# A bidirectional hybrid encoder layer: half of the first gather made during routing, and whole-expert loads in the last loop

## The reference

```python
scores = jax.nn.sigmoid(x2d @ w_router)              # 256 x 64
choice = scores + router_bias
grp_score = lax.top_k(choice.reshape(T, 8, 8), 2)[0].sum(-1)
_, top_groups = lax.top_k(grp_score, 4)              # 4 of 8 groups
_, idx = lax.top_k(jnp.where(emask, choice, -jnp.inf), 8)
wsel = wsel / wsel.sum(-1, keepdims=True) * ROUTED_SCALE
...
h = jax.nn.silu(xb @ w_gate[e]) * (xb @ w_up[e])     # 1024 -> 256
out = (h @ w_down[e]) * gate[:, None]                # 256 -> 1024
y = y.at[tok].add(out)
...
shared = (jax.nn.silu(x2d @ ws_gate) * (x2d @ ws_up)) @ ws_down
```

## Time and profile before

| | before |
|---|---|
| median of 3 runs | 745.39 us (743.74, 745.39, 745.47) |
| the profiled execution | 744.41 us |
| its span | 742.5 us |
| PE busy, share of the span | 96% |
| DVE, ACT, POOL busy | 35%, 22%, 6% |
| HBM read | 249.27 MB |
| mean granted TensorE clock | 0.993 |

### The profile page before, as it was taken

One profiled execution on the slowest core, in us unless ns is written; L12 is line 12 of the kernel. 1 busy time (PEld: TensorE's weight loads), 2 busy tenths in 40 slices (PEclk: granted clock), 3 DMA queues, 4 the chain that ended last, 5 costly groups with the idle time before them and its releaser, 6 DMA issues.

```text
span 742.5 us, 11168 instructions
## 1 busy us (share of the span) xinstructions
PE 715.2 (96%) x4520; PEld 416.7 (56%) x4520; DVE 260.8 (35%) x639; ACT 164.9 (22%) x345; POOL 48.0 (6%) x65
## 2 busy tenths in 40 slices
PE   7999999999999999999999999999998999999993
PEld 6888888888864455444444445444443445444441
DVE  3401599656757085222112121022211122112225
ACT  1010423407950043211211111111111121111111
POOL 0120020320320020100000000000000000000000
PEclk9999999999999999999999999999999999999998
DMA  8963544544399548999999999999999999999993
GB/s 329 408 210 147 173 169 167 175 169 159 125 375 376 226 160 332 359 391 423 428 418 429 423 432 429 433 426 421 434 425 422 427 430 419 429 425 421 417 405 157
DMA packets 30931, 250.98 MB, mean 338 GB/s; under 512 B 4001, under 2 KB 4785, under 8 KB 10017
## 3 DMA queue, kind: packets, MB, share of 16 engines
q1 hardware_dynamic: 27792, 240.78, 79.3%
q0 software_dynamic: 2432, 8.44, 3.3%
q10 hardware_dynamic: 656, 1.05, 0.5%
HBM read 249.27 MB, written 1.11 MB: 337 GB/s over the span
## 4 chain that ended last, share of the span: by engine, by line
PE 77%; DVE 9%; SPq 6%; DMA 6%; issue 1%; ACT 1%; DVEq 0%
PE bank L1194 22%; PE bank L820 16%; PE bank L1262 9%; PE bank L1112 8%; PE bank L963 7%; DMA arena<-in_we_dram 5%; PE bank L1132 5%; DVE arena L1585 5%; SPq L627 3%; PE bank L934 1%; PE bank L900 1%; SPq L636 1%; PE bank L1236 1%; PE bank L1271 1%; ACT bank L1350 1%
## 5 line engine op out<-in xcount | busy, mean ns | idle before, releaser
L1194 PE MATMUL bank<-arena 128*64 128x512 f32 (+2 forms) x1008 | 198.7, 601 | 3.7 <-DMA arena<-in_we_dram 3.7
L820 PE MATMUL bank<-arena 128*128 128x256 f32 x768 | 167.7, 379 | 0.0
L820 PEld LDWEIGHTS bank<-arena 128*128 128x128 f32 x768 | 145.6, 190 | 20.5 <-issue 0.4
L1194 PEld LDWEIGHTS bank<-arena 128*64 128x64 f32 (+2 forms) x1008 | 57.7, 127 | 95.6 <-issue 92.9
L1262 PE MATMUL bank<-arena 128*64 128x512 f32 (+2 forms) x512 | 91.7, 584 | 3.3 <-DMA arena<-in_we_dram 1.8
L1112 PEld LDWEIGHTS bank<-onehotb,h_part 128*128 128x128 bf16 x1248 | 69.9, 98 | 20.1 <-issue 20.0
L1112 PE MATMUL bank<-onehotb,h_part 128*128 128x128 bf16 x1248 | 74.3, 219 | 0.2 <-DVE onehotb L1815 0.2
L1903 DVE TENSOR_TENSOR y_lo<-bank,y_hi 128x512 fp32r<-128x512 f32 (+1 forms) x51 | 34.7, 680 | 101.8 <-ACT y_hi L1495 75.5
L1880 DVE TENSOR_REDUCE arena<-bank 64x1 f32<-64x3 f32 (+1 forms) x64 | 10.1, 158 | 160.4 <-PE bank L1212 159.8
L1262 PEld LDWEIGHTS bank<-arena 128*64 128x64 f32 (+1 forms) x512 | 26.2, 124 | 53.7 <-issue 44.6
L963 PE MATMUL bank<-arena 128*128 128x512 f32 x128 | 55.3, 592 | 0.0
(11 more groups left out here) (274 smaller groups left out, 489.8 us busy)
## 6 DMA issues: line engine op xcount, KB each, us to landing
arena<-in_we_dram SPq DMA_DIRECT2D x82, 1024.0 KB, 17.9
arena<-in_we_dram SPq DMA_DIRECT2D x17, 3072.0 KB, 30.2
arena<-in_we_dram SPq DMA_DIRECT2D x22, 2048.0 KB, 30.7
arena<-in_wc_dram SPq DMA_DIRECT2D x15, 1024.0 KB, 11.4
arena<-in_wn_dram SPq DMA_DIRECT2D x8, 1024.0 KB, 4.7
arena<-in_wo_dram SPq DMA_DIRECT2D x8, 1024.0 KB, 4.8
apart<-in_we_dram SPq DMA_DIRECT2D x7, 1024.0 KB, 27.9
arena<-decay_rows POOLq DMA_DIRECT2D x5, 1024.0 KB, 7.1
```

The lines of the kernel that those rows point to most:

```text
L820: mm = nc.tensor.matmul(bank[n % 2][:, j * S:(j + 1) * S], wk, xk, start=(k == 0), stop=(k == KD - 1))
L1194: mm = nc.tensor.matmul(bank[0][rows[q], :], hc[v][:, k, rows[q]], place[at_q[part][q]][:, c:c + 512], start=(k == 0), stop=(k == KD - 1))
```

## The change

**Routing.** The ranks of the first half of the tokens are made as soon as their experts are chosen, in a bank of their own (bank 7). `before` now has 256 on its diagonal, so that a chosen token's rank comes out of the matmul already marked, and the one-hot of a half can be made by one VectorE instruction from PSUM (`first_one_hot`). The one for t = 0 stands inside `top_k(1)`; the first half's 24 matmuls of gather 0 (`gather_of(0, ...)`) are issued while `top_k(1)` runs. After the second ranks come its one-hot and the other 24. The matmuls of `idle_front` go, but for the first 6. `prefixes` moves from the middle of the gather to behind it, and is now float32, with its two matrices loaded with `pk`; `jobs_b` and its cast go. `token_tables` moves from before k = 0 to k = 2 of batch 0, and `job_tables` from k = 2 to k = 3. The h residuals' matmuls use banks 4 and 5.

**Loads.** In the loop each expert of batches 21 to 25 is one load of its three thirds (two, where its places are not side by side); batch 26 keeps single thirds and pieces. And SP waits, for each load, only for the place that is given back last.

```diff
-TABLES_K = 2
-PREFIX_K = 2
-ROUTE_PE = (6, 1, 3)
+TABLES_K = 3
+ROUTE_PE = 6
...
             if closes(b, turn) or (turn is None and b < PAIRED_FROM):
                 return [[(part, q)] for part in range(PARTS) for q in range(w)]
-            if turn is not None or b < WHOLE_FROM:
+            if turn is None and b < WHOLE_FROM:
                 return [[(0, q), (1, q)] for q in range(w)] + [[(2, q)] for q in range(w)]
             return [[(part, q) for part in range(PARTS)] for q in range(w)]
...
+        def waits_for(b, turn, parts, q):
+            if turn is None:
+                return [max(parts, key=lambda p: given_back[True, b, p, q])]
+            return sorted({max(parts, key=lambda p: given_back[at, b, p, q]) for at in (False, None)})
...
-                    for p, _ in whole[::-1]:
-                        if turn is not None or uses(b, turn, p, q):
-                            sp.wait_ge(free[home(b, turn, p, q)], uses(b, turn, p, q))
+                    for p in waits_for(b, turn, [p for p, _ in whole], q):
+                        sp.wait_ge(free[home(b, turn, p, q)], uses(b, turn, p, q))
...
+            def ranks(t):
+                pe.wait_ge(sel_bf, t + 1)
+                to = bank[7][:, 0:E] if t == 0 else bank[3][:, 0:E]
+                for i in range(t + 1):
+                    mm = nc.tensor.matmul(to, (before if i == t else onesb)[:], selb[:, i, :],
+                                          start=(i == 0), stop=(i == t))
+                mm.then_inc(rank_ready, 1)
...
-                if half == 1:
-                    idle_front(ROUTE_PE[1])
...
-            idle_front(ROUTE_PE[2])
             pe.wait_ge(h_part2, 2 * T)
             pe.wait_ge(onehot_ready, 1)
-            gather(0, 0, within=PREFIX_K)
-            gather(0, 1)
-            token_tables()
+            for half in range(2):
+                gather_of(1, half).then_inc(gather_ready, 1)
+            prefixes()
...
+                    if first and k == TABLES_K - 1:
+                        token_tables()
...
+            def first_one_hot(t, marked_rank):
+                dve.wait_ge(rank_ready, t + 1)
+                return V.scalar_tensor_tensor(out=onehotb[0][:, t, :].rearrange("p (e m) -> p e m", e=2),
+                                              in0=marked_rank.unsqueeze(2).to_broadcast([P, 2, M]), scalar=-255.0,
+                                              in1=iota[:, 0:M].unsqueeze(1).to_broadcast([P, 2, M]),
+                                              op0=ALU.add, op1=ALU.is_equal)
...
+                if t == 1:
+                    first_one_hot(0, bank[7][:, 0:2]).then_inc(first_hot, 1)
...
-            one_hot(0, 0, 2, rk, slice(0, 2))
-            V.tensor_copy(jobs_b[0:E, :], jobs).then_inc(jobs_ready, 1)
+            V.tensor_copy(number_b[0:E, 0:1], expert).then_inc(jobs_ready, 1)
```

More of the change, by code:

```diff
@@ L207, in build @@
         o_pk = O_ST
-        pk = at(o_pk, NPK + 2 * NJ, rows=E)
+        pk = at(o_pk, NPK + 2 * NJ + 2 * E, rows=E)
         pk_iota = pk[:, NPK:NPK + NJ]
-        pk_steps = pk[:, NPK + NJ:]
-        o_pk += NPK + 2 * NJ
+        pk_steps = pk[:, NPK + NJ:NPK + 2 * NJ]
+        pk_ahead, pk_all = [pk[:, NPK + 2 * NJ + i * E:NPK + 2 * NJ + (i + 1) * E] for i in range(2)]
+        o_pk += NPK + 2 * NJ + 2 * E
         pc = at(o_pk, 32, rows=E)
@@ L500, in take @@
                 spot[(turn is None, b) + third] = (at_c, fills[at_c], first, signals[first])
+                given_back[(turn is None, b) + third] = user.get(at_c, (-1, -1, -1))
+                last = b + (shared(b, turn) == 0) + (0 if turn is None else FIRST_B)
+                user[at_c] = (last, *third)
                 fills[at_c] += 1
@@ L523, in build @@
                 take(0, b, whole)
+        for b in range(TURN_B):
+            for load in order[False, b]:
+                for third in load:
+                    at_c = spot[(False, b) + third][0]
+                    given_back[(None, b) + third] = user[at_c]
+                    user[at_c] = (b + FIRST_B + TURN_B, *third)
         for part in range(PARTS):
@@ L1018, in idle_front @@
                 for i in range(count):
-                    nc.tensor.matmul(bank[7][:, :], identb[:], h_part[0][:, 0, 0:512], start=True, stop=True)
+                    nc.tensor.matmul(bank[0][:, :], identb[:], h_part[0][:, 0, 0:512], start=True, stop=True)
             transposes(0)
@@ L1023, in _, with gather_of @@
             pe.wait_ge(h_part0, 1)
-            idle_front(ROUTE_PE[0])
+            idle_front(ROUTE_PE)
             transposes(1)
             logits(1)
+            def ranks(t):
[5 more added lines that the diff above has]
+                mm.then_inc(rank_ready, 1)
+            def gather_of(t, half):
+                for k in range(4 * half, 4 * half + 4):
+                    for i in range(3):
+                        mm = nc.tensor.matmul(bank[1 + half][:, (k % 4) * P:(k % 4 + 1) * P],
+                                              h_part[i][:, t, k * P:(k + 1) * P], onehotb[0][:, t, :],
+                                              start=(t == 0 and i == 0 and k % 4 == 0), stop=(t == T - 1 and i == 2),
+                                              skip_group_check=True)
+                return mm
             pe.wait_ge(consts_ready, 2)
+            pe.wait_ge(s_vec, 64)
             for half in range(2):
@@ L1031, in _ @@
                 pe.wait_ge(h_part0, T + half + 1)
-                nc.tensor.matmul(bank[half][:, :], ident[:], h[:, 1, c], start=True, stop=False)
-                nc.tensor.matmul(bank[half][:, :], nidentb, h_part[0][:, 1, c], start=False, stop=True
+                nc.tensor.matmul(bank[4 + half][:, :], ident[:], h[:, 1, c], start=True, stop=False)
+                nc.tensor.matmul(bank[4 + half][:, :], nidentb, h_part[0][:, 1, c], start=False, stop=True
                                  ).then_inc(rest_ready, 1)
+                if half == 0:
+                    ranks(0)
+            pe.wait_ge(h_part2, T)
             for half in range(2):
                 c = slice(half * 512, (half + 1) * 512)
-                if half == 1:
-                    idle_front(ROUTE_PE[1])
                 pe.wait_ge(h_part1, T + half + 1)
-                nc.tensor.matmul(bank[half][:, :], nidentb, h_part[1][:, 1, c], start=False, stop=True,
+                nc.tensor.matmul(bank[4 + half][:, :], nidentb, h_part[1][:, 1, c], start=False, stop=True,
                                  skip_group_check=True).then_inc(rest_ready, 1)
[L1043 to L1050, removed]
+                if half == 0:
+                    pe.wait_ge(first_hot, 1)
+                    gather_of(0, 0)
+            ranks(1)
             for i in range(T):
@@ L1105, in gate_tables, with gather @@
                 mm.then_inc(rank_table, 1)
-            def gather(v, half, within=None):
+            def gather(v, half):
                 for k in range(4 * half, 4 * half + 4):
@@ L2017, in layout @@
     out["negm"] = np.stack([np.where(s <= t, 0, NEG), np.where(s >= t, 0, NEG)], 1).astype(f)
-    out["before"] = (s < t).astype(f)
+    out["before"] = (s < t) + 256 * np.eye(P, dtype=f)
     out["convw"] = v["conv_w"][0][:, xbc_order].reshape(TAPS, CT, P).transpose(2, 1, 0).reshape(P, CT * TAPS)
```

29 lines of the change are left out of this document (15 added, 14 removed).

## The result

| | before | changed |
|---|---|---|
| median of 6 runs each, same chip | 745.43 us (743.74 to 746.63) | 748.78 us (747.63 to 748.95) |
| ratio, 95% interval | | 1.0039 (1.0024 to 1.0055) |
| profiled execution, and its span | 744.41, 742.5 | 748.81, 747.0 |
| mean granted clock of TensorE | 0.993 | 0.989 |
| TensorE idle for loads of gate and up, and of down | 3.7 and 1.8 us | 9.1 and none |

By the medians the changed kernel is 3.35 us slower; the ratio gives 2.9 us, between 1.8 and 4.1. The medians are a little beyond what can be told from no change. I start with the list of what TensorE waited for, in the changed kernel (total us, times, longest).

What follows compares the result with a forecast made beforehand. The prediction took loads as the bound at 564 and 729 us, with TensorE and DMA both full from 300 us. Routing -0.6, wait less given back +1.4, clock +1.7 made +2.5 on the mean 744.87: 747.4 us, range 743.7 to 748.8.

Steps and rivals of the forecast that it cites:

- Routing: Routing stage, 270 to 291 us: +0.3 on the chain, -0.93 for one k less behind the job tables; -0.6 us.
- The wait at batch 23: Head of narrow batch 23: TensorE waits for the last whole expert, 24 MiB in 59.2 us; 3.2 us (2.8 to 4.4).
- No other wait in the loop: Batches 22 and 24: their loads are whole before TensorE comes, so neither start waits.
- The clock: After the wait at batch 23: TensorE's granted clock falls as it did at 561 us, costing +1.7 us.
- Given back: Down in batch 26: its three waits for loads go, returning 1.8 of the 3.2 us, leaving +1.4 us.
- The sum: Whole run: -0.6 + 1.4 + 1.7 = +2.5 us, giving 747.4 us; chance 0.40.
- The clock holds: Rival at batch 23: same wait, but the clock stays up; +0.8 us, 745.9 us; chance 0.27.
- Faster: Rival in the loop: batch 23 is complete when TensorE comes, for instance by faster large loads; 743.0 us; chance 0.12.
- Within the reserve: Rival at batch 23: the wait is under 1.8 us, so only routing counts; 744.8 us; chance 0.13.
- The costly routing: Rival in routing: it ends 0.4 us later; with the wait and the clock +3.5, 748.6 us; chance 0.08.

Runs made afterwards that it cites:

- narrow alone: The changed kernel, but of the loop's batches only the narrow batch 23 loads whole experts, the wide ones as before: 748.42 us, ratio 1.0039.
- the unread matmuls: The changed kernel with 14 matmuls that nobody reads on TensorE at the head of batch 23, ahead of its wait for the load: 747.32 us, ratio 1.0020.
- loads alone: The kernel before with whole experts in the loop and SP's shorter list of waits, routing as before: 748.99 us, ratio 1.0046.
- only the wide batches: The changed kernel with whole experts in wide batches 21, 22, 24 and 25, narrow batch 23 loaded in parts as before: 746.68 us, ratio 1.0008.
- only the first two: The changed kernel with whole-expert loads only in batches 21 and 22; 23, 24 and 25 as before: 745.06 us, ratio 0.9989.
- before with the unread matmuls: The kernel before with the same kind of 14 unread matmuls ahead of the wait at the head of batch 17: 745.79 us, ratio 1.0006.
- routing alone: The changed kernel with the loop's loads and SP's waits of before, so the routing edit only: 745.38 us, ratio 0.9991.
- SP's waits alone: The changed kernel with loads in the form before, keeping the routing edit and SP's shorter list of waits: 745.34 us, ratio 0.9997.

## Why the prediction was right, and where its sizes were off

**Routing.** The instants that the prediction named came as forecast, less the 0.8 us: job tables 288.1 (forecast 288.1), first load 290.8 (290.8), batch 0 at 284.0 (284.1), the copy of the prefixes 284.1 (284.06), a half one-hot 0.29 (0.3). The idle ahead of the job tables came out at 0.87, about the 0.8 left between 287.3 and 288.1. One agreement has some luck in it. The prediction had 24 matmuls of the gather run beside `top_k(1)`, at no cost, and 24 behind the one-hot from 282.2. Only 12 ran there. The other 12 stood behind the second ranks and ran on into the last 24 (x36, 2.18 us, from 282.35 - 0.8 = 281.55), so that TensorE didn't wait for the one-hot at all. Both ways end at 283.7 to 283.8. What -0.6 us of stage is worth in the run was measured only as -0.35 us (-0.7 by the ratio) with zero inside the interval. So the stage's gain is shown, its value at the end is not.

**The wait at batch 23.** Place and releaser were right. For the 24 MiB the prediction took 59.2 us from 428 GB/s. Between the landings of the same two loads it was 58.6 in the changed kernel's trace, 58.9 in narrow alone, 59.4 with the unread matmuls and 60.1 in loads alone, which all have batch 23 joined, and 60.3 where only the wide batches or only the first two are; with all of the loop's loads apart it was 60.4 in before and 60.0 in before with the unread matmuls, but 59.2 in routing alone and in SP's waits alone. So 59.2 lies in the scatter, and the two forms can't be told apart: the 424 against 428 GB/s of the earlier trace rows, which the prediction read as a small effect of size, is no more than that.

The length of the wait was 4.82 instead of 3.2, the bounds being 2.8 to 4.4. Two things make up the difference, both visible. TensorE was through with its gather at 668.38 - 4.82 = 663.6; the forecast puts it at 664.4 - 0.6 + 0.8 = 664.6 in the time of this execution. It came 1.0 earlier, since batch 17 went at full clock (+1.7) but itself began 0.7 later than forecast (565.23 against 564.34 - 0.6 + 0.8). The last expert landed at 668.24 against 667.7, 0.5 later, since the stream was 1.2 us later at 609.7 and then a little faster. The prediction had said that a wait is longer by as much where the clock holds at 565, with the same end; that is the larger part. Where the clock did fall at 17, as forecast, the wait was 4.02 (loads alone) and 4.33 (narrow alone), inside the bounds but longer than 3.2.

**No other wait in the loop.** Right for this kernel. It holds only because TensorE is late from the wait at 23, as the wide batches alone showed.

**The clock.** It fell, as said. The term was 1.7 us, taken from the earlier trace rows; the stretch from batch 23 to 24 lost 2.1 here, as more of the 40 rows of gate and up ran at the low clock (6.71 us instead of 4.43). In this execution the term was 0.4 too small; over the three traces with the fall, 1.2, 2.1 and 2.6, it is of the right size.

**Given back.** Forecast 1.8: batch 26's last piece of down starts at 733.50 against 729.09, +4.4, while batch 23 was +4.0 (668.38 against 664.41) and the clock +2.1 more. 4.0 + 2.1 - 4.4 = 1.7, with the three waits gone.

**The sum.** In the profiled executions 4.0 + 2.1 - 1.7 = +4.4, which is 748.81 - 744.41. Of it 0.8 was there at 46 us. The remaining 3.6 stand against +2.5 forecast: 0.6 from the later start of batch 23, 0.4 from the clock, 0.1 given back less. The medians say +3.35, the ratio +2.9. The mechanism and the direction were right, and the forecast of 747.4 was 1.4 us low: about 0.85 from the sum and 0.55 from its base, the mean 744.87 of three runs, where the six of the result have a median of 745.43.

The 0.6 is there at batch 17 already (565.23 against 564.54), ahead of the loop's loads: from 17 to 23 the forecast had 667.6 - 564.34 = 103.3 us, and it took 103.2. What a single execution does at that place is scatter: batch 17 started between 564.34 and 567.00 in before, the changed kernel and the loads alone, which have the same loads up to there, and at 562.76 in SP's waits alone. That also hides the -0.6 us by which the prediction shifts the whole stream. The distance from batch 17 to 23 is steadier: 103.2 us changed, 104.0 loads alone, 104.4 narrow alone, 104.0 with the unread matmuls. In before it is 100.1, with no wait for that load.

**The rivals.** *The clock holds* failed: it fell in all three profiles of kernels with an unfilled wait at 23, and where the wait was filled the stretch was 2.2 us shorter. *Faster* failed on its own point: it needed 24 MiB in 56.1 us, and no trace had them under 58.6. *Within the reserve* failed, with 4.8, 4.0 and 4.3 against 1.8. *The costly routing* gave nearly the measured time, 748.6, but for the wrong reason: alone, that edit costs nothing that can be told.

**What stays open.** The value of the routing edit between none and about 1 us. Why the clock fell behind 2.50 us in one variant and behind 3.21 in narrow alone, but not behind 3.21 at the same place in the changed kernel. How much of the loss is the fall and how much the wait, more sharply than 1.4 and 1.5 us: no kernel was run with the clock held at both batch 17 and 23.

## What to carry to other kernels

Where the DMA engines were full all the time, joining loads of 1 and 2 MiB into 3 changed no rate that could be told (24 MiB in 58.6 to 60.3 us with some or all joined, 59.2 to 60.4 apart); it changed what landed when. So set up for each batch when the last part that its first instruction needs has landed, and when the engine arrives there, without counting the waits that the change itself would put ahead: join loads in the batches that have the lead, and leave apart those that don't. A stall that is hidden by a later wait, a lower clock too, is no longer hidden when that later wait is gone.

## What the runs showed of the hardware beyond that

- The clock fell to 0.50 behind TensorE idles of 2.50 us (batch 24, only the wide batches whole), of 2.94 to 3.33 and 4.20 at batch 17 in eight kernels, and of 4.02, 4.33 and 4.82 at batch 23. It did not fall behind 3.21 us at batch 17 in the changed kernel, where the same 3.21 in narrow alone was enough. Idles up to 1.54 us (only the wide batches whole, at 435 us) left it up.
- A fall cost 6.21 - 4.51 = 1.7 us at batch 17 in six of the profiled executions, and in two the same 20 rows took 7.30 (unread matmuls at 23) and 7.46 (SP's waits alone), 2.8 and 2.9 us more. 14 unread bf16 matmuls, 3 us, held it in the two places where they were tried.
